# A one-core hybrid decoder step: the down-projection weights of 31 experts are issued from ScalarE's DMA queue

## What is computed

```python
# _hmoe: every row picks one group of four, then two of its eight experts
# _grouped_experts, for a block of rows xb of expert e, all float32, 1024 wide:
def expert(args):
    xb, e = args
    hmid = jax.nn.silu(xb @ w1[e]) * (xb @ w3[e])
    return hmid @ w2[e]
```

## Time and profile before

| | us |
|---|---|
| median of 3 runs | 1853.34 |
| lowest, highest | 1847.88, 1853.68 |
| span of the profiled execution | 1850.1 |
| busy: PE / DVE / ACT / POOL | 1528.6 / 521.4 / 270.3 / 56.6 |

### The profile page before, as it was taken

One profiled execution on the slowest core, in us unless ns is written; L12 is line 12 of the kernel. 1 busy time (PEld: TensorE's weight loads), 2 busy tenths in 40 slices (PEclk: granted clock), 3 DMA queues, 4 the chain that ended last, 5 costly groups with the idle time before them and its releaser, 6 DMA issues.

```text
span 1850.1 us, 18498 instructions
## 1 busy us (share of the span) xinstructions
PE 1528.6 (83%) x7041; PEld 668.8 (36%) x7041; DVE 521.4 (28%) x1010; ACT 270.3 (15%) x606; POOL 56.6 (3%) x71
## 2 busy tenths in 40 slices
PE   6999989899899989959877787778778787777781
PEld 3445456564344554533222222222222222222220
DVE  2065855541222241343112121212112121212125
ACT  2123235411111131200000000000000000000001
POOL 3000000000000000000000000000000000000002
PEclk9999976789898999969999899998989898999996
DMA  7312220365831237359999999999999999999995
GB/s 281 115 46 87 75 69 1 97 228 202 300 116 57 91 114 254 147 202 411 410 410 410 411 410 410 410 411 410 411 410 410 411 410 411 410 410 410 411 392 195
DMA packets 153031, 521.45 MB, mean 282 GB/s; under 512 B 10048, under 2 KB 10608, under 8 KB 152976
## 3 DMA queue, kind: packets, MB, share of 16 engines
q1 hardware_dynamic: 134912, 468.48, 64.8%
q0 software_dynamic: 10096, 37.01, 5.6%
q10 hardware_dynamic: 7968, 15.21, 2.2%
HBM read 496.94 MB, written 23.72 MB: 281 GB/s over the span
## 4 chain that ended last, share of the span: by engine, by line
PE 46%; DMA 33%; SPq 9%; DVE 8%; ACT 2%; issue 2%; POOL 0%; ACTq 0%; DVEq 0%; POOLq 0%
DMA ring<-w 31%; PE psum L2347 11%; PE psum L1892 10%; PE psum L1880 7%; SPq L643 4%; SPq L648 3%; PE psum L2059 3%; PE psum L2370 2%; PE psum L1978 2%; SPq L654 1%; PE psum L1865 1%; DVE ring L1349 1%; PE psum L1997 1%; PE psum L2208 1%; PE psum L2231 1%
## 5 line engine op out<-in xcount | busy, mean ns | idle before, releaser
L2347 PE MATMUL psum<-ring,r_c 128*64 128x512 f32 x1536 | 406.7, 686 | 137.1 <-DMA ring<-w 135.9
L2370 PE MATMUL psum<-ring,r_c 128*64 128x512 f32 x1024 | 240.0, 604 | 68.4 <-DMA ring<-w 54.7
L2347 PEld LDWEIGHTS psum<-ring,r_c 128*64 128x64 f32 x1536 | 119.3, 157 | 421.2 <-DMA ring<-w 212.0
L1796 DVE TENSOR_SCALAR r_c<-r_c 128x512 f32<-128x512 f32 x32 | 13.7, 427 | 798.1 <-ACT r_c L1147 798.1
L2370 PEld LDWEIGHTS psum<-ring,r_c 128*64 128x64 f32 x1024 | 70.6, 137 | 217.3 <-issue 111.2
L1880 PE MATMUL psum<-r_h,ring 128*128 128x512 f32 x320 | 139.0, 595 | 0.0
L1892 PE MATMUL psum<-ring,r_h 128*128 128x512 f32 x256 | 115.1, 610 | 5.0 <-DMA ring<-w_in 3.8
L1147 ACT ACTIVATE r_c<-psum 128x512 f32<-128x512 f32 x32 | 19.1, 598 | 630.6 <-PE psum L2347 630.6
L1798 DVE RECIPROCAL r_c<-r_c 128x512 f32<-128x512 f32 x32 | 107.3, 3352 | 1.1
L1880 PEld LDWEIGHTS psum<-r_h,ring 128*128 128x128 f32 x320 | 60.6, 191 | 75.4 <-issue 75.4
L1892 PEld LDWEIGHTS psum<-ring,r_h 128*128 128x128 f32 x256 | 49.5, 196 | 65.9 <-issue 65.7
(11 more groups left out here) (340 smaller groups left out, 1373.0 us busy)
## 6 DMA issues: line engine op xcount, KB each, us to landing
ring<-w SPq DMA_DIRECT2D x320, 1024.0 KB, 18.7
r_h<-w SPq DMA_DIRECT2D x32, 1024.0 KB, 19.4
r_mix<-w SPq DMA_DIRECT2D x32, 1024.0 KB, 19.8
ring<-w_in SPq DMA_DIRECT2D x7, 2048.0 KB, 10.5
ring<-cache_moba_v SPq DMA_DIRECT2D x32, 256.0 KB, 5.0
ring<-cache_mem_k POOLq DMA_DIRECT2D x8, 1024.0 KB, 7.3
ring<-cache_mem_v SPq DMA_DIRECT2D x8, 1024.0 KB, 9.3
out_rows<-r_c ACTq DMA_DIRECT2D x64, 128.0 KB, 5.9
```

The source lines that it names most:

```text
L2347: ins = pe.matmul(psum[2 + 2 * u + m][CAP * half:CAP * (half + 1), :], xT[:, k, CAP * u:CAP * (u + 1)], moe_place(2 * q + m, u)[:, kk, 512 ...
L2370: ins = pe.matmul(psum[7][CAP * half:CAP * (half + 1), :], heT[u][:, k % 4, CAP * (k // 4):CAP * (k // 4 + 1)], ring[:, 8 + q, kk, 512 * h ...
```

## The change

SP no longer issues the chunks 8 to 11 of any expert but the first. ACT does: in `down`, behind its wait for all four chunks of this expert's `down` and ahead of the copy out of PSUM, it issues the four chunks of the next expert.

```diff
@@ block.sync
                     first_weights(e, n + 2, 1 - n, e + (n + 2))
                     up_weights(e, n + 1, e + (n + 1))
-                    down_weights(e, n, e + n, (9, 8, 10, 11) if n else (8, 9, 10, 11))
             first_weights(0, NE - 1, 1, NE - 1)
             up_weights(0, NE - 2, NE - 2)
-            down_weights(0, NE - 3, NE - 3)
             up_weights(0, NE - 1, NE - 1)
-            down_weights(0, NE - 2, NE - 2)
-            down_weights(0, NE - 1, NE - 1)
@@ block.scalar
-            def down(j, c):
+            def down(j, c, weights=True):
                 u = c % 2
                 act.wait_ge(ht_full, 2 * j + (c + 1))
                 act.activation(heT[u].rearrange("p c t -> p (c t)"), psum[6], ACT.Copy).then_inc(ht_free, 1)
                 act.wait_ge(down_used, 8 * j + 4 * (c + 1))
+                if weights:
+                    for r in range(8, 12):
+                        act.dma_start(moe_place(r, 0), moe_chunk(r, 2 * j + (c + 1))).then_inc(wm_in[r], 16)
                 if reused(j, c):
                     act.wait_ge(rows_in[u], 32 * (j if c >= 0 else j - 1))
                 act.activation(ys[u], psum[7], ACT.Copy).then_inc(y_free, 1)
...
-            down(NE // 2 - 1, 1)
+            down(NE // 2 - 1, 1, weights=False)
```

More of the change, by code:

```diff
@@ L648, in up_weights, with down_weights @@
                     sp.dma_start(moe_place(r, 0), moe_chunk(r, expert)).then_inc(wm_in[r], 16)
[L650 to L653, removed]
+            def down_weights(b, n, expert):
+                for r in range(8, 12):
+                    sp.wait_ge(down_used, 4 * b + (4 * n + r - 11))
                     sp.dma_start(moe_place(r, 0), moe_chunk(r, expert)).then_inc(wm_in[r], 16)
@@ L1189, in _ @@
                             gate_exp(j, u)
-                            down(j, u)
+                            down(j, u, weights=False)
                         for u in range(2):
```

## The result

The changed kernel takes 1861.5 us in the median (1856.8 to 1868.6, 10 runs) against 1853.1 for the kernel before (10 runs): a ratio of 1.0048, 95% interval 1.0032 to 1.0065, so 6 to 12 us slower. The forecast was 1864.3 us, +11.0. The profiled executions differ by 9.7 us, spans of 1859.8 and 1850.1.

What follows compares the result with a forecast made beforehand. The prediction took DMA bytes at 410 GB/s to bound the experts. Middle 0, plus 7.7 and 3.3 us at the end, gave +11.0 us on 1853.3, so 1864.3 us, range 1851 to 1885.

Steps and rivals of the forecast that it cites:

- The term 0 for the middle: Stretch from 822 to 1794 us: no change, as the bytes stay, if some request is always open.
- The estimate of half: ACT's queue gets half the rate, 205 GB/s; four chunks take 20.5 us, leaving about 7 us to spare per expert.
- The starved queue: Rival: ACT's queue gets below 36% in the expert loop, down comes late; +25 to +90 us, about 1905 us; chance 0.11.
- Step 1: At the end, until down(29) ends: 1786.1 us instead of 1778.35, +7.7 us (0 to 9.6).
- Step 2: From the end of down(29) to that of down(30): 22.14 us before, change 0, with 2.5 us of cover.
- Step 3: From the end of down(30) to that of down(31), requested from idle DMA engines: 14.6 us instead of 11.32, +3.3 us.
- The rival that nothing would be lost at the end: down(29) ends as early as before and only 2.6 to 3.3 us remain at the end: 1856 us; chance 0.13.
- The rate did not rise: Denies the rival that two queues move more together over the 972 us: 420 GB/s, -12 us, 1841 us; chance 0.09.

Runs made afterwards that it cites:

- experiment 1: Changed kernel, but the down chunks of experts 29 to 31 go back to SP in the old order: 1851.6 us against 1852.3 for the kernel before.
- the second profile: The unmodified changed kernel run and profiled again beside the kernel before on the same chip: ratio 1.0045 (1.0028 to 1.0063).
- experiment 3: Kernel before, with only expert 31's down chunks issued by ACT, four at once after down(30): ratio 1.0027 (1.0009 to 1.0046).
- experiment 2: Kernel before, with only the down chunks of experts 29 to 31 issued by ACT, four at once: 1868.2 us, ratio 1.0078.
- experiment 5: Changed kernel, but ACT issues each next down chunk once the same chunk of this down is used: 1865.6 us, ratio 1.0057.

## Why the prediction was right

**What bounds it.** 410 GB/s from the first expert to the last stretch, before and after, and experiment 1 puts the loop's own cost at 0 within 0.2%. The term 0 for the middle holds.

**Sharing.** The estimate of half was right: up chunks 5.12 us apart is 205 GB/s. ACT's four chunks take 24.8 us from the first issue to the last landing in the row of down(28) above, and 24.6 to 25.1 us in 27 of the loop's 29 sets by the trace's semaphores. With the last chunk's matmuls that is 26.7 us, 2 to 3 more than the working had, of a period of 32: 5 us to spare, not 7. The starved queue did not come; how little ACT's queue could have before it does was not tried. The Trainium skill's rule of turns between queues ("DMA: Bandwidth & Descriptors", "Queues, rings and completion order") agrees with the 5.12 us, half of the rate for each. The sentence of the Trainium skill that several issuing engines save only the issuing time (same page, "Issuing engines are not separate DMA queues") holds here for the rate, 410 on either side, but not for the time: the second queue changes the order in which bytes come.

**Step 1, +7.7 forecast, +6.35 measured** (1784.70 against 1778.35), +9.7 in the second profile. The last chunk of up(30) was there at 1773.03, 2.8 us earlier than the forecast 1775.8. The working had 13.1 MB left behind it; there were 13.9:

```profile
1773.00:1822.00 49.00, 42.48 (x180) 13.89 (x180) 10.30 (x8) 4.63 (x8) 0.00 (x0) 0.90 0.73 284
```

284 GB/s x 49 us is 13.9 MB, worth 2.0 us of the 2.8. The working's list left out the last two chunks of down(29): by the trace's semaphores they land at 1774.30 and 1779.42, so "whose chunks are there by then" does not hold for the fourth, which comes after down(29) has begun (1777.62). It cost nothing, since PE turns to it only near 1782.9. The 1.0 us for landing came from no row either: the one named leaves 1.8 (4.9 less 2.56 and 0.5), and no run parts it into before and after the transfer. The chunk's matmuls took 3.2 us (1773.08 to the transposes at 1776.27) instead of 1.87, at a granted clock of 0.59, which gave 1.3 back. That the errors are of opposite sign is luck, and so is part of the closeness of the sum. The reason behind the step holds: in the old order down(29) uses each chunk as it lands and ends 2 us after the last; in the new one PE reaches down(29) only after the last up chunk, which has shared the rate with down chunks, and the 11.6 us from there to the end of down(29) hold no wait for a chunk.

**Step 2, 0**: 22.12 us against 22.14. **Step 3, +3.3 forecast, +3.34 measured** (1806.82 to 1821.48 is 14.66 us, 11.32 before), and 3.3 us in experiment 3 (down(30) to down(31) 14.64). PE waited for the first chunk for 4.94 us, the row of one chunk into idle engines. It then ran at a granted clock of 0.50 to 1816 us, but the last chunk set the end, as forecast: its weight load still waited for it at 1819.52, 12.7 us after the request, where the working had 12.6.

**ACT.** Four issues in 2.0 to 2.7 us at the end, 2.2 forecast; the late copy, the late stores and the exponential behind them cost nothing.

**Sum.** +9.7 us by the profiles, +11.0 forecast, and a median 8.5 us up. The rival that nothing would be lost at the end rested on step 1 being 0; it was not. The rate did not rise.

## What to carry to other kernels

Bytes set the pace here, and a second queue added no rate (410 GB/s either way); it changed the order in which bytes arrive. The two full queues shared half and half, so what is needed later came at the expense of what is needed next. In the loop this cost nothing (experiment 1); it was paid at the end (experiment 2), where the work that was put off has few loads left beside it. So cost such a change at its end: which request is made last, what releases it, and how much work still follows the last chunk.

## What the runs showed that was not expected

Two executions of one kernel differed by 2.7 us in a stretch of 12 to 14 us, with the granted clock at 0.68 and 0.88. Over the middle, 900 to 1700 us, the changed kernel has a granted clock of 0.90 against 0.92; PE's more frequent short waits are not shown to be the cause, since experiment 1, with the same loop and as many waits there (67), has 0.92. And asking for chunks earlier, as in experiment 5, did not make the end earlier.
